# Decode attention: the value product with 128 stationary columns, its lower half added on VectorE, and the last head's inverse issued ahead of the value pages

## The chip, the cores and the metric

One core of one Trainium2 chip runs the whole kernel. The metric is the device time of one execution in microseconds; the median of three runs of the kernel before is 2565.19 us.

## What is computed

One inference step of a small decoder trunk in float32, for a prompt of 1040 rows (1024 and 16 learned ones) and for 8 sequences of 4 new tokens each, called the samples here: a short gated convolution layer with a squared-ReLU MLP, then a layer of attention with forget gates, again with an MLP. The change lies in the attention of the samples. Each sample sequence has 256 cached keys and values in two pages of 128 rows, and 4 new ones:

```python
def forget_attention(q, k, v, c_q, c_k, q_pos, k_pos):
    s = jnp.einsum('nqhd,nkhd->nhqk', q, k, preferred_element_type=jnp.float32) * (HEAD_DIM ** -0.5)
    s = s + (jnp.transpose(c_q, (0, 2, 1))[:, :, :, None] - jnp.transpose(c_k, (0, 2, 1))[:, :, None, :])
    causal = k_pos[None, :] <= q_pos[:, None]
    s = jnp.where(causal[None, None], s, NEG_INF)
    p = jax.nn.softmax(s, axis=-1)
    return jnp.einsum('nhqk,nkhd->nqhd', p.astype(v.dtype), v)
...
past_v = gather_pages(cache_v, page_table)
y = attend(q, ctx).reshape(N, T, ATTN_DIM) @ w_o[j]
```

With 16 heads and 4 queries there are 64 rows of probabilities for each sequence.

## The kernel before, in words

The program is written by hand for each engine, with semaphores between them. Activations stand transposed, features on partitions. TensorE works in the float32r format; to keep accuracy each operand is split into a high part (ScalarE rounds it) and a low part (VectorE subtracts), and a product is made as high by high, low by high and high by low.

**Around the change.** The prompt's attention runs head by head; its last step for a head is to send the sums of the exponentials through memory, to invert them, and to divide. SP does this: `spread_sums` (L1563) spreads the sums over partitions, VectorE inverts them in `invert_sums` (L1279), `load_inverse` stores the inverse (L1570), waits until it is stored, and loads it back broadcast over 64 partitions (L1573). VectorE then divides (`divide`, L1286), ScalarE rounds the result (`o_split_hi`, L1498), VectorE cuts its low part (`o_split_lo`, L1503). After head 15 SP loads the new values, then the two value pages of sequence 0 (`load_v_pages`, L1597), then the inverse of head 15.

After that the output projection of the prompt runs on TensorE: eight units of eight steps, each step six matmuls of 358 columns (L591). Between its steps `decode_step` puts the work of the samples by a table: seven steps are one round. In round n TensorE

- turns the keys of sequence n in four parts (`d_turn_keys`, L1300, four transposes each), at the steps 0, 2 and 4 and, for the last part, between the two halves of the value product;
- turns the probabilities of sequence n-1 at step 2 (`d_turn_probs`, L1415);
- at step 4 multiplies them with the values (`d_weigh`, L1460 and L1462), 512 output columns at a time;
- at step 6 turns the output (`d_turn_out`, L1477) and then makes the logits of sequence n (`d_logits`, L1362 to L1366).

Each part of the keys has one bank: ScalarE rounds it (`d_keys_hi`, L1325), VectorE cuts the low part (`d_keys_lo`, L1330) and so frees the bank for the next part. The logits already use 128 stationary columns, high and low queries side by side; ScalarE copies the lower half of the result (`d_cross`, L1372), and VectorE adds it (L1381) on the way to the maximum (L1383). Then ScalarE takes the exponential (`d_exp`, L1391) and VectorE normalises (`d_norm`, L1398 to L1404).

The probabilities, turned, lie in one PSUM tile as 2 pages and 1 block of new keys, 64 columns each. `d_probs_hi` (L1423) rounds all of it, `d_probs_lo` (L1428, L1432) cuts the low parts. `d_weigh` takes for each page three matmuls (high by high, low by high, high by low) and one for the new keys: seven for a half, 14 for a sequence. `d_keep` (L1469) copies both halves to `d_out`. The value pages are rounded by `d_values_hi` (L1438) and cut by `d_values_lo` (L1445); of the new values the low part is cut at L1892.

**The order on each engine** is that of the code. In rounds 1 to 4 VectorE goes, after the keys of sequence n and the low queries: `add_prompt` (L1964, the sum of the projection's unit into the residual), `cut_unit` (L575, the low part of the weights of the unit after the next), `d_values_lo` (L1445), `d_max`. In rounds 5 to 7 `add_prompt` and `cut_unit` come behind `d_values_lo`. Round 8 only finishes sequence 7. ScalarE goes in rounds 1 to 4: keys, queries, rounding of the weights (L567), `d_keep`, `d_values_hi`, `d_output` (L1491).

Of the kernel before, what the change touches and what calls it, by code (L numbers as in the profile page):

```python
# [215 lines left out]
def trunk(nc, a, out):  # L216

    ctx = ExitStack()
    with ctx:
# [203 lines left out]
        DPL = put("d_probs_t_lo", [P, NPAGE, HQ], F32R)  # L423
# [10 lines left out]
        DPH = put("d_probs_t_hi", [P, NPAGE + 1, HQ], F32R)  # L434
# [78 lines left out]
        dw_done, dw_kept, do_done, do_used = sem("dw_done"), sem("dw_kept"), sem("do_done"), sem("do_used")  # L513
        o_hi, o_lo, rest_hi, rest_lo = sem("o_hi"), sem("o_lo"), sem("rest_hi"), sem("rest_lo")
# [904 lines left out]
        def d_probs_hi(b):  # L1419

            act.wait_ge(dp_done, b + 1)
            ge(act, dw_done, 2 * b)
            act.activation(DPH[:, :, :].rearrange("p g r -> p (g r)"), ps_probs(), ACT.Copy).then_inc(dp_hi, 1)  # L1423

        def d_probs_lo(b):

            dve.wait_ge(dp_hi, b + 1)
            dve.tensor_tensor(DPL[:, :, :].rearrange("p g r -> p (g r)"), ps_probs()[:, 0:NPAGE * HQ],  # L1428
                              DPH[:, 0:NPAGE, :].rearrange("p g r -> p (g r)").bitcast(F32), ALU.subtract)\
               .then_inc(dp_used, 1)  # L1430
            low = DPH[NS:2 * NS, NPAGE, :]
            dve.tensor_tensor(low, ps_probs()[NS:2 * NS, NPAGE * HQ:], low.bitcast(F32), ALU.subtract).then_inc(dp_used, 1)  # L1432
# [15 lines left out]
        def d_weigh(b, h):  # L1448

            if h == 0:  # L1450
                if b == 0:
                    pe.wait_ge(acc_free, 3 * HEADS)
                    pe.wait_ge(vn_lo, 1)
                pe.wait_ge(dv_lo, NPAGE * (b + 1))
                pe.wait_ge(dp_used, 2 * b + 2)
                ge(pe, dw_kept, 2 * b)
            f = slice(512 * h, 512 * h + 512)
            for g in range(NPAGE):
                for n in range(3):
                    pe.matmul(PS[0:HQ, D_OUT + h, :], (DPL if n == 1 else DPH)[:, g], (VPL if n == 2 else VPH)[:, g, f],  # L1460
                              start=(g == 0 and n == 0), stop=False)
            pe.matmul(PS[0:HQ, D_OUT + h, :], DPH[0:3 * NS, NPAGE], VD[:, f], start=False, stop=True).then_inc(dw_done, 1)  # L1462

        def d_keep(b):

            ge(act, do_done, b)
            for h in range(2):
                act.wait_ge(dw_done, 2 * b + h + 1)
                act.activation(OD[:, 512 * h:512 * h + 512], PS[0:HQ, D_OUT + h, :], ACT.Copy).then_inc(dw_kept, 1)  # L1469
# [58 lines left out]
        def attention_loaders(stage_out):  # L1528
# [87 lines left out]
            def prompt_loads():  # L1616
# [24 lines left out]
                for x in range(3):  # L1641
                    sp.dma_start(VN[NS * x:NS * x + NS, :], out["v_sample"].rearrange("b t h d -> (b t) (h d)"))\
                      .then_inc(vn_loaded, 16)
                load_v_pages(0)
                load_inverse(HEADS - 1)
# [76 lines left out]
        def attention_scalar(square, root, inverse, stage_hi):  # L1722
# [57 lines left out]
            d_values_hi(0)  # L1780
# [4 lines left out]
            d_exp(0)  # L1785
            d_keys_hi(1, 1)
# [46 lines left out]
        def attention_vector(head_lo, head_fin, stage_lo):  # L1833
# [56 lines left out]
            dve.wait_ge(vn_hi, 1)  # L1890
            low = VD[2 * NS:3 * NS, :]
            dve.tensor_tensor(low, VN[2 * NS:3 * NS, :], low.bitcast(F32), ALU.subtract).then_inc(vn_lo, 1)  # L1892
# [3 lines left out]
            d_norm(0)  # L1896
            d_values_lo(0, 0)
            d_keys_lo(1, 1)
            d_values_lo(0, 1)
            for n in range(1, DB):  # L1900
# [8 lines left out]
                if n <= 4:  # L1909
                    add_prompt(n - 1)  # L1910
                    cut_unit(U_O + n + 1)
                d_values_lo(n)
# [13 lines left out]
            cut_unit(U_O + DB)  # L1926
            dve.wait_ge(rest_hi, KC + 1)
# [1354 lines left out]
```

## Time and profile before

| | |
|---|---|
| runs | 2564.46, 2565.19, 2565.80 us |
| profiled execution | 2564.02 us, its span 2561.7 us |
| TensorE (PE) matmul busy | 2525.1 us, 99% of the span |
| VectorE (DVE) busy | 1808.4 us, 71% |
| ScalarE (ACT) busy | 1048.2 us, 41% |
| mean granted clock of TensorE | 0.999 of full speed |
| the rounds of the samples | about 1690 to 1830 us |
| value product, L1460 and L1462 | 112 matmuls of 512 columns |

A row of a timeline has its start and its length in us from the start of the span; matmuls overlap in their lengths, so what one costs is read from start to start. "Idle before" names who ended the wait. PE is the matmul side of TensorE and PEld its weight load, which runs ahead of the matmul; SPq is the DMA queue of SyncE.

### The profile page before, as it was taken

The page shows a single profiled execution, that of the slowest core. Times are in us where ns is not written, and L with a number is a line of the kernel's source. Part 1 is how long each engine was busy: PE and PEld are TensorE (multiplying, and loading weights), DVE is VectorE, ACT ScalarE, POOL GpSimd, SP SyncE. Part 2 cuts the span into 40 slices and gives each one's busy share as a digit, 9 for nine tenths or more (in the row PEclk, how much of TensorE's full clock was granted, in tenths as well). Part 3 has the DMA queues.
Part 4 walks back from the last instruction along what each step waited for, and adds up shares of the span by engine and source line. Part 5 has one row for each costly group of instructions (what it writes and reads, how often), then busy time and mean ns, then how long its engine had stood idle before and what let it go on. Part 6 is the DMA issues. An engine that isn't in the chain of part 4 may idle for free.

```text
span 2561.7 us, 45919 instructions
## 1 busy us (share of the span) xinstructions
PE 2525.1 (99%) x18332; PEld 2473.7 (97%) x18332; DVE 1808.4 (71%) x2438; ACT 1048.2 (41%) x1491; POOL 24.4 (1%) x48
## 2 busy tenths in 40 slices
PE   8999999999999999999999999999999999999998
PEld 8999999999999999999999899988899999999998
DVE  5434437666688998954345898876696666899986
ACT  4111124333333323465245777765553333333333
POOL 0000000000000000000000100000000000000000
PEclk9999999999999999999999999999999999999999
DMA  3111111332353312025424656644223333433111
GB/s 120 50 41 48 43 43 40 124 101 101 102 197 105 129 63 90 6 83 168 118 77 137 141 136 167 145 127 148 92 84 101 101 101 108 178 135 135 51 51 69
DMA packets 248430, 259.42 MB, mean 101 GB/s; under 512 B 18160, under 2 KB 182960, under 8 KB 248290
## 3 DMA queue, kind: packets, MB, share of 16 engines
q1 hardware_dynamic: 229030, 248.37, 31.1%
q10 hardware_dynamic: 19260, 9.09, 1.3%
q8 instruction: 100, 1.64, 0.3%
q14 instruction: 40, 0.33, 0.0%
HBM read 193.86 MB, written 63.42 MB: 100 GB/s over the span
## 4 chain that ended last, share of the span: by engine, by line
PE 87%; DVE 4%; DMA 3%; ACT 2%; issue 2%; SPq 2%; ACTq 0%; DVEq 0%
PE ps L591 28%; PE ps L790 24%; PE ps L845 24%; PE ps L810 2%; DMA sums_spread<-o_and_sums 1%; PE ps L1252 1%; PE ps L1102 1%; PE ps L1167 1%; PE ps L1254 1%; PE ps L1253 1%; PE ps L1169 1%; PE ps L1460 1%; PE ps L629 1%; PE ps L692 1%; DMA inv_rows<-inv_spread 0%
## 5 line engine op out<-in xcount | busy, mean ns | idle before, releaser
L845 PE MATMUL ps<-h_op,w_op 128*128 128x268 f32 x4912 | 615.1, 286 | 2.7 <-DVE w_op L885 2.5
L845 PEld LDWEIGHTS ps<-h_op,w_op 128*128 128x128 f32 x4912 | 610.4, 189 | 3.4 <-DVE w_op L885 3.4
L591 PE MATMUL ps<-x_hi,w_hi 128*128 128x358 f32 x1248 | 277.2, 330 | 4.9 <-DVE w_lo L575 4.7
L575 DVE TENSOR_TENSOR w_lo<-w_raw,w_hi 128x1024 fp32r<-128x1024 f32 x76 | 92.8, 1221 | 257.2 <-ACT w_hi L567 257.2
L591 PE MATMUL ps<-x_hi,w_lo 128*128 128x358 f32 x1248 | 273.3, 327 | 0.0
L591 PE MATMUL ps<-x_lo,w_hi 128*128 128x358 f32 x1248 | 272.9, 327 | 0.0
L856 ACT ACTIVATE w_op<-w_op_f 128x2048 fp32r<-128x2048 f32 (+1 forms) x54 | 97.7, 1809 | 388.4 <-PE ps L845 367.6
L591 PEld LDWEIGHTS ps<-x_hi,w_hi 128*128 128x128 f32 x1248 | 213.7, 190 | 7.1 <-DVE w_lo L575 5.1
L591 PEld LDWEIGHTS ps<-x_lo,w_hi 128*128 128x128 f32 x1248 | 215.9, 189 | 0.0
L591 PEld LDWEIGHTS ps<-x_hi,w_lo 128*128 128x128 f32 x1248 | 215.6, 189 | 0.0
L1040 DVE TENSOR_TENSOR t<-ps,t 128x536 f32<-128x536 f32 x180 | 128.7, 715 | 120.2 <-PE ps L790 111.4
L567 ACT ACTIVATE w_hi<-w_raw 128x1024 fp32r<-128x1024 f32 x76 | 80.0, 1054 | 295.2 <-PE ps L591 291.0
L971 DVE TENSOR_TENSOR acc<-ps,acc 128x536 f32<-128x536 f32 x256 | 174.2, 706 | 14.3 <-PE ps L845 13.9
L885 DVE TENSOR_TENSOR h_op<-h_op_f,h_op 128x2144 fp32r<-128x2144 f32 (+1 forms) x56 | 125.9, 2248 | 43.1 <-ACT h_op L856 43.1
L790 PE MATMUL ps<-x_hi,a_lo 128*128 128x268 f32 x720 | 148.3, 287 | 0.0
L790 PE MATMUL ps<-x_T_hi,s_lo 128*128 128x268 f32 x720 | 147.7, 286 | 0.0
L1008 ACT ACTIVATE t<-t 128x536 f32<-128x536 f32 x90 | 58.9, 654 | 184.7 <-DVE t L1014 184.7
L885 DVE TENSOR_TENSOR w_op<-w_op_f,w_op 128x2048 fp32r<-128x2048 f32 (+1 forms) x54 | 115.7, 2142 | 0.0
L790 PEld LDWEIGHTS ps<-x_hi,a_lo 128*128 128x128 f32 x720 | 112.9, 189 | 0.0
L790 PEld LDWEIGHTS ps<-x_T_hi,s_lo 128*128 128x128 f32 x720 | 112.5, 189 | 0.0
L1211 DVE TENSOR_TENSOR probs_lo<-probs_f,probs_hi 128x768 fp32r<-128x768 f32 (+3 forms) x128 | 98.1, 766 | 20.2 <-ACT probs_hi L1199 10.6
L856 ACT ACTIVATE h_op<-h_op_f 128x2144 fp32r<-128x2144 f32 (+1 forms) x56 | 104.5, 1869 | 7.9 <-DVE h_op_f L933 7.8
(358 smaller groups left out, 5173.6 us busy)
## 6 DMA issues: line engine op xcount, KB each, us to landing
raw_a<-in_mlp_w SPq DMA_DIRECT2D x120, 256.0 KB, 3.1
h_op_f<-h_rows SPq DMA_DIRECT2D x24, 1072.0 KB, 6.2
w_op_f<-in_mlp_w SPq DMA_DIRECT2D x24, 1024.0 KB, 7.5
h_rows<-t SPq DMA_DIRECT2D x90, 268.0 KB, 2.1
w_raw<-in_conv_w_in SPq DMA_DIRECT2D x24, 512.0 KB, 3.7
w_raw<-in_w_kv SPq DMA_DIRECT2D x16, 512.0 KB, 4.7
w_raw<-in_w_o SPq DMA_DIRECT2D x16, 512.0 KB, 3.9
k_page<-in_cache_k SPq DMA_DIRECT2D x16, 512.0 KB, 5.1
```

The costliest lines, as they stand in the source:

```text
L567: act.activation(WH[:, s], RAW[:, s], ACT.Copy).then_inc(w_hi, 1)
L575: dve.tensor_tensor(WL[:, s], RAW[:, s], WH[:, s].bitcast(F32), ALU.subtract).then_inc(w_lo, 1)
L591: mm = pe.matmul(PS[:, bank(s, g), 0:GW], w[:, s, k], x[:, k, g * GW:(g + 1) * GW], start=(k == 0 and n == 0), stop=(k == KC - 1 and n == 2))
L790: mm = pe.matmul(PS[:, 2 * p + g, 0:QW], w[:, k], x[:, k, g * QW:(g + 1) * QW], start=(k == 0 and j == 0), stop=(k == KC // 2 - 1 and j == 2))
L810: mm = pe.matmul(PS[:, 2 * p + g, 0:QW], w[:, k, P * m:P * m + P], x[:, k, a:a + QW], start=(k == 0 and j == 0), stop=(k == UNIT_TILES - 1 ...
L845: mm = pe.matmul(PS[:, 2 * p + g, 0:QW], w[:, k, P * m:P * m + P], x[:, k, QW * g:QW * g + QW], start=(k == 0 and j == 0), stop=(k == tile ...
L856: act.activation(h_flat(to, n), h_flat(raw, n), ACT.Copy).then_inc(second_hi, 1)
L885: dve.tensor_tensor(h_flat(pieces[1], n), h_flat(raw, n), h_flat(pieces[0], n).bitcast(F32), ALU.subtract) .then_inc(second_lo, 1)
L971: mm = dve.tensor_tensor(two(to), pair(PAIRS2[l][i]), two(to), ALU.add)
L1008: act.activation(UB[USLOT[q]], UB[USLOT[q]], ACT.Square).then_inc(hf_done, 1)
L1040: dve.tensor_tensor(two(to), pair(p), two(other), ALU.add).then_inc(m_read, 1)
L1211: dve.tensor_tensor(PBL[:, t % HI_RING, 0:nb * w], PF[:, t % 2, 0:nb * w], PBH[:, t % HI_RING, 0:nb * w].bitcast(F32), ALU.subtract).then_ ...
```

## The change

Three things are edited.

1. High and low probabilities of the two pages stand side by side in one tile (`DPT`, 128 columns a page), those of the new keys in a tile of their own (`DPN`). ScalarE rounds them in two instructions where it was one. `d_weigh` takes the high part of a page's values with all 128 columns in one matmul, whose rows 64 to 127 are the low probabilities' share: five matmuls for a half, ten for a sequence.
2. `d_keep` copies rows 64 to 127 instead of rows 0 to 63, and a new `d_sum` on VectorE adds rows 0 to 63 to that copy, for each half of 512 columns. `d_turn_out` waits for it. `d_sum` stands ahead of `d_values_lo` in every round, and behind `add_prompt` and `cut_unit` in rounds 1 to 4 and in round 8.
3. For head 15 `load_inverse` is issued ahead of `load_v_pages(0)`. On ScalarE the rounding of the first pages moves behind the first exponential; on VectorE the cut of the new values' low part (L1892) moves behind the first normalising.

```diff
-        DPL = put("d_probs_t_lo", [P, NPAGE, HQ], F32R)
+        DPN = put("d_probs_t_new", [P, HQ], F32R)
...
-        DPH = put("d_probs_t_hi", [P, NPAGE + 1, HQ], F32R)
+        DPT = put("d_probs_t_hi_lo", [P, NPAGE, 2 * HQ], F32R)
...
         def d_probs_hi(b):
...
-            act.activation(DPH[:, :, :].rearrange("p g r -> p (g r)"), ps_probs(), ACT.Copy).then_inc(dp_hi, 1)
+            act.activation(DPT[:, :, 0:HQ], ps_probs()[:, 0:NPAGE * HQ].rearrange("p (g r) -> p g r", r=HQ), ACT.Copy)\
+               .then_inc(dp_hi, 1)
+            act.activation(DPN[:, :], ps_probs()[:, NPAGE * HQ:], ACT.Copy).then_inc(dp_hi, 1)
...
         def d_weigh(b, h):
...
-            for g in range(NPAGE):
-                for n in range(3):
-                    pe.matmul(PS[0:HQ, D_OUT + h, :], (DPL if n == 1 else DPH)[:, g], (VPL if n == 2 else VPH)[:, g, f],
-                              start=(g == 0 and n == 0), stop=False)
-            pe.matmul(PS[0:HQ, D_OUT + h, :], DPH[0:3 * NS, NPAGE], VD[:, f], start=False, stop=True).then_inc(dw_done, 1)
+            out, pairs = PS[0:HQ, D_OUT + h, :], PS[0:2 * HQ, D_OUT + h, :]
+            pe.matmul(pairs, DPT[:, 0], VPH[:, 0, f], start=True, stop=False)
+            pe.matmul(out, DPT[:, 0, 0:HQ], VPL[:, 0, f], start=False, stop=False)
+            pe.matmul(out, DPT[:, 1, 0:HQ], VPL[:, 1, f], start=False, stop=False)
+            pe.matmul(out, DPN[0:3 * NS, :], VD[:, f], start=False, stop=False)
+            pe.matmul(pairs, DPT[:, 1], VPH[:, 1, f], start=False, stop=True).then_inc(dw_done, 1)
...
         def d_keep(b):
...
-                act.activation(OD[:, 512 * h:512 * h + 512], PS[0:HQ, D_OUT + h, :], ACT.Copy).then_inc(dw_kept, 1)
+                act.activation(OD[:, 512 * h:512 * h + 512], PS[HQ:2 * HQ, D_OUT + h, :], ACT.Copy).then_inc(dw_cross, 1)
+
+        def d_sum(b):
+
+            for h in range(2):
+                dve.wait_ge(dw_cross, 1 + 2 * b + h + 1)
+                x = OD[:, 512 * h:512 * h + 512]
+                dve.tensor_tensor(x, PS[0:HQ, D_OUT + h, :], x, ALU.add).then_inc(dw_kept, 1)
...
+                load_inverse(HEADS - 1)
                 load_v_pages(0)
-                load_inverse(HEADS - 1)
...
             act.activation(VD[:, :], VN[:, :], ACT.Copy).then_inc(vn_hi, 1)
-            d_values_hi(0)
...
             d_exp(0)
+            d_values_hi(0)
...
-            dve.wait_ge(vn_hi, 1)
-            low = VD[2 * NS:3 * NS, :]
-            dve.tensor_tensor(low, VN[2 * NS:3 * NS, :], low.bitcast(F32), ALU.subtract).then_inc(vn_lo, 1)
             o_split_lo(KC - 1)
             d_max(0)
             d_keys_lo(1, 0)
             d_norm(0)
+            dve.wait_ge(vn_hi, 1)
+            low = VD[2 * NS:3 * NS, :]
+            dve.tensor_tensor(low, VN[2 * NS:3 * NS, :], low.bitcast(F32), ALU.subtract).then_inc(vn_lo, 1)
             d_values_lo(0, 0)
...
                 if n <= 4:
                     add_prompt(n - 1)
                     cut_unit(U_O + n + 1)
+                d_sum(n - 1)
                 d_values_lo(n)
...
             cut_unit(U_O + DB)
+            d_sum(DB - 1)
```

The order of VectorE's instructions in rounds 1 to 4, from the cut of the last two parts of the keys (L1330) to the maximum. Before:

```order
L1330 TENSOR_TENSOR k_t_lo<-ps,k_t_hi 128x4x128 x2
L1344 TENSOR_TENSOR q_blocks_hi_lo<-q_all,q_blocks_hi_lo 64x8x4 x2
L1346 SCALAR_TENSOR_TENSOR sums_lo<-past_sums,sums_hi 16x288
L1964 TENSOR_TENSOR acc<-ps,acc 128x716
L575 TENSOR_TENSOR w_lo<-w_raw,w_hi 128x1024
L1445 TENSOR_TENSOR v_page_lo<-v_page,v_page_hi 128x2048
L1381 TENSOR_TENSOR mask_and_cross<-mask_row,d_cross 64x288
```

The same place with the change (its line numbers are its own):

```order
L1331 TENSOR_TENSOR k_t_lo<-ps,k_t_hi 128x4x128 x2
L1345 TENSOR_TENSOR q_blocks_hi_lo<-q_all,q_blocks_hi_lo 64x8x4 x2
L1347 SCALAR_TENSOR_TENSOR sums_lo<-past_sums,sums_hi 16x288
L1976 TENSOR_TENSOR acc<-ps,acc 128x716
L576 TENSOR_TENSOR w_lo<-w_raw,w_hi 128x1024
L1479 TENSOR_TENSOR d_out<-ps,d_out 64x512 x2
L1447 TENSOR_TENSOR v_page_lo<-v_page,v_page_hi 128x2048
```

Two sums (L1479) stand between the cut of the weights and the cut of the value pages.

TensorE between the turning of the keys and the turning of the output (`d_out`), with the change; before, each half had seven matmuls of 64 stationary columns:

```order
L1461 MATMUL ps<-v_page_hi,d_probs_t_hi_lo 128x512
L1462 MATMUL ps<-v_page_lo,d_probs_t_hi_lo 64x512
L1463 MATMUL ps<-v_page_lo,d_probs_t_hi_lo 64x512
L1464 MATMUL ps<-v_new_hi_hi_lo,d_probs_t_new 64x512
L1465 MATMUL ps<-v_page_hi,d_probs_t_hi_lo 128x512
L1301 MATMUL ps<-ident,k_page 128x128 x4
```

The first and last matmul of a half now write 128 rows; the last turning of the keys still stands between the halves.

VectorE from the division of the last heads (L1286) to the value pages, before:

```order
L1286 TENSOR_TENSOR q_all<-o_and_sums,inv_sums 64x1040 x2
L1892 TENSOR_TENSOR v_new_hi_hi_lo<-v_new,v_new_hi_hi_lo 32x1024
L1503 TENSOR_TENSOR hid_lo<-q_all,hid_hi 128x716
L1381 TENSOR_TENSOR mask_and_cross<-mask_row,d_cross 64x288
...
L1404 TENSOR_SCALAR d_probs<-d_probs,d_stats 64x288
L1445 TENSOR_TENSOR v_page_lo<-v_page,v_page_hi 128x1024
```

and with the change:

```order
L1287 TENSOR_TENSOR q_all<-o_and_sums,inv_sums 64x1040 x2
L1513 TENSOR_TENSOR hid_lo<-q_all,hid_hi 128x716
L1382 TENSOR_TENSOR mask_and_cross<-mask_row,d_cross 64x288
...
L1405 TENSOR_SCALAR d_probs<-d_probs,d_stats 64x288
L1906 TENSOR_TENSOR v_new_hi_hi_lo<-v_new,v_new_hi_hi_lo 32x1024
L1447 TENSOR_TENSOR v_page_lo<-v_page,v_page_hi 128x1024
```

The cut of the new values has moved from ahead of L1503 to behind the normalising.

## Rows read from the trace of the kernel before

**Rows 1.** Waits, 1680 to 1850 us: who waited, total us, times, longest

```profile
PE ps L591 <- DVE hid_lo L1503: 3.0, 2, 2.7
PEld ps L1300 <- DVE k_t_lo L1330: 2.0, 7, 0.3
```

**Rows 2.** Timeline of TensorE, round 2: start us, length us, instruction

```profile
1729.54 0.39 PE L1462 MATMUL ps<-v_new_hi_hi_lo,d_probs_t_hi 96*64 96x512 f32 x1
1729.77 0.62 PE L1300 MATMUL ps<-ident,k_page 128*128 128x128 f32 x4
...
1731.61 0.40 PE L1462 MATMUL ps<-v_new_hi_hi_lo,d_probs_t_hi 96*64 96x512 f32 x1
...
1733.91 0.71 PE L1477 MATMUL ps<-ident,d_out 64*128 64x64 f32 x8
```

**Rows 3.** Timeline of VectorE, round 2

```profile
1728.98 0.69 DVE L1330 TENSOR_TENSOR k_t_lo<-ps,k_t_hi 128x512 fp32r<-128x512 f32 x1 [1.29 <-ACT k_t_hi L1325]
...
1732.70 0.88 DVE L1964 TENSOR_TENSOR acc<-ps,acc 128x716 f32<-128x716 f32 x1
1733.52 1.20 DVE L575 TENSOR_TENSOR w_lo<-w_raw,w_hi 128x1024 fp32r<-128x1024 f32 x1
```

**Rows 4.** Timeline of ScalarE, round 2

```profile
1728.35 0.60 ACT L1325 ACTIVATE k_t_hi<-ps 128x512 fp32r<-128x512 f32 x1 [2.10 <-PE ps L1300]
...
1732.71 1.05 ACT L1469 ACTIVATE d_out<-ps 64x512 f32<-64x512 f32 x2
1733.67 1.90 ACT L1438 ACTIVATE v_page_hi<-v_page 128x2048 fp32r<-128x2048 f32 x1
```

**Rows 5.** Timeline of SP's DMA queue: stores and loads of the inverses, heads 14 and 15

```profile
1686.69 0.35 SPq L1570 DMA_DIRECT2D inv_rows<-inv_spread  x1
1688.04 0.48 SPq L1573 DMA_DIRECT2D inv_sums<-inv_rows  x1
...
1695.33 0.44 SPq L1570 DMA_DIRECT2D inv_rows<-inv_spread  x1
1699.45 0.48 SPq L1573 DMA_DIRECT2D inv_sums<-inv_rows  x1
```

**Rows 6.** The value pages' tile: time of their 16 loads

```profile
DMA to landing us min/median/max: 3.2/5.1/5.7
```

**Rows 7.** Timeline of VectorE, ahead of round 1

```profile
1693.90 0.23 DVE L1279 RECIPROCAL inv_spread<-sums_spread 65x16 f32<-65x16 f32 x1
...
1699.64 1.23 DVE L1286 TENSOR_TENSOR q_all<-o_and_sums,inv_sums 64x1040 f32<-64x1040 f32 x1
1702.84 1.24 DVE L1286 TENSOR_TENSOR q_all<-o_and_sums,inv_sums 64x1040 f32<-64x1040 f32 x1 [1.97 <-DMA inv_sums<-inv_rows]
1704.00 1.21 DVE L1892 TENSOR_TENSOR v_new_hi_hi_lo<-v_new,v_new_hi_hi_lo 32x1024 fp32r<-32x1024 f32 x1
1705.24 0.91 DVE L1503 TENSOR_TENSOR hid_lo<-q_all,hid_hi 128x716 fp32r<-128x716 f32 x1
...
1712.79 0.69 DVE L1330 TENSOR_TENSOR k_t_lo<-ps,k_t_hi 128x512 fp32r<-128x512 f32 x1
```

**Rows 8.** Timeline of TensorE, ahead of round 1 and in it

```profile
1706.20 0.59 PE L591 MATMUL ps<-hid_hi,w_hi 128*128 128x358 f32 x2 [2.73 <-DVE hid_lo L1503]
...
1713.78 0.60 PE L1300 MATMUL ps<-ident,k_page 128*128 128x128 f32 x4
```

**Rows 9.** Timeline of TensorE, rounds 5 and 6

```profile
1777.81 0.62 PE L1300 MATMUL ps<-ident,k_page 128*128 128x128 f32 x4
...
1781.98 0.71 PE L1477 MATMUL ps<-ident,d_out 64*128 64x64 f32 x8
...
1789.64 0.36 PE L1415 MATMUL ps<-ident,d_probs 64*128 64x64 f32 x3 [0.21 <-DVE d_probs L1404]
```

**Rows 10.** Start of the kernel: TensorE's timeline, and the busy-time table (last: clock, DMA)

```profile
21.71 1.23 PE L591 MATMUL ps<-x_hi,w_hi 128*128 128x358 f32 x3 [4.47 <-DVE w_lo L575]
...
20.00:30.00 10.00, 8.29 (x41) 8.29 (x42) 10.00 (x11) 8.92 (x10) 0.00 (x0) 0.83 0.19 54
```

More of the change, by code:

```diff
@@ L513, in trunk @@
         dw_done, dw_kept, do_done, do_used = sem("dw_done"), sem("dw_kept"), sem("do_done"), sem("do_used")
+        dw_cross = lt_kept
         o_hi, o_lo, rest_hi, rest_lo = sem("o_hi"), sem("o_lo"), sem("rest_hi"), sem("rest_lo")
@@ L1422, in d_probs_hi @@
             ge(act, dw_done, 2 * b)
-            act.activation(DPH[:, :, :].rearrange("p g r -> p (g r)"), ps_probs(), ACT.Copy).then_inc(dp_hi, 1)
+            act.activation(DPT[:, :, 0:HQ], ps_probs()[:, 0:NPAGE * HQ].rearrange("p (g r) -> p g r", r=HQ), ACT.Copy)\
+               .then_inc(dp_hi, 1)
+            act.activation(DPN[:, :], ps_probs()[:, NPAGE * HQ:], ACT.Copy).then_inc(dp_hi, 1)
         def d_probs_lo(b):
[L1427 to L1431, printed above, removed]
+            dve.wait_ge(dp_hi, 2 * b + 2)
+            dve.tensor_tensor(DPT[:, :, HQ:2 * HQ], ps_probs()[:, 0:NPAGE * HQ].rearrange("p (g r) -> p g r", r=HQ),
+                              DPT[:, :, 0:HQ].bitcast(F32), ALU.subtract).then_inc(dp_used, 1)
+            low = DPN[NS:2 * NS, :]
             dve.tensor_tensor(low, ps_probs()[NS:2 * NS, NPAGE * HQ:], low.bitcast(F32), ALU.subtract).then_inc(dp_used, 1)
```

## Prediction

> **What bounds the kernel now.** I started from the busy shares on the page: TensorE is busy nearly all the time, so a matmul taken out looks like time gained. That is an average, though, so I went to the one stretch that the change touches, from about 1690 to 1830 us, and read there first the list of waits, then the timelines of the engines side by side. The waits show two things [rows 1]. TensorE waits once for long, 2.7 us for the low half of head 15's output (L1503). And its weight loader waits seven times 0.3 us at L1300 for the low half of the keys (L1330): once a round, hidden under a running matmul, so with no slack left behind it. I call "round n" the seven steps in which TensorE weighs the values of sequence n-1 and turns the keys of sequence n; T is the start of the round's last turning of keys (L1300 between the two halves of the value product). T is 1729.77 in round 2 and 1777.81 in round 5 [rows 2, 9].
>
> **Part 1: fewer matmuls in the value product.** Seven matmuls of 512 columns per half become five; 2 x 2 x 8 = 32 go. One takes 0.23 us: from the last of a half at 1729.54 to the L1300 behind it at 1729.77 [rows 2]. On TensorE alone that is 32 x 0.23 = 7.4 us. Where do they lie?
>
> *First half, rounds 1 to 7.* L1300 at T needs the bank that L1330 frees. In round 2 ScalarE rounds the turning before it from 1728.35, L1330 runs 1728.98 to 1729.67, and T is 1729.77 [rows 2 to 4]. TensorE's own product ended exactly then. With two matmuls less TensorE is there 0.46 us earlier and waits 0.46 us for the same L1330. T does not move: gain 0. (Two matmuls by 0.23 are hidden by the chain ScalarE, VectorE; without that chain they would be worth 0.46 us a round.)
>
> *Second half, rounds 1 to 7.* It shortens the way from T to the turning of the output (L1477), which then stands at a new wait, part 2.
>
> *Round 8* has no keys to turn; its four removed matmuls count in full, 4 x 0.23 = 0.93 us, since the new adds are covered there: ScalarE's copy of half a row block (1.05 us for two, [rows 4]) and one add (0.69) make some 1.3 us against the 2.3 us between the last value matmul, 1731.61, and L1477, 1733.91 [rows 2]. **-0.9 us.**
>
> **Part 2: the added sum on VectorE.** ScalarE now copies the low rows (same size, same place in its order), and VectorE adds the high rows, twice 64 x 512 out of PSUM; only then may L1477 start. The trace has no such add. The nearest row is L1330, also 512 elements with one side in PSUM: 0.69 us [rows 3]. Two, with the 0.06 us by which neighbours overlap (L1964 starts at 1732.70, takes 0.88, and L575 starts at 1733.52), are 1.32 us. Bounds: 1.1 and 1.5 us.
>
> What counts is where VectorE takes them. In rounds 1 to 4 the order puts them behind the prompt's sum (L1964) and the cut of the next weights (L575), ahead of the value pages. L575 starts at T + 3.75 and takes 1.20 [rows 3]; the sums run from T + 4.88 to T + 6.20, and L1477 follows some 0.1 us later, at **T + 6.3**. Today it is at T + 4.14 [rows 2], right behind ScalarE's copies (1732.71 plus 1.05, that is T + 3.99, [rows 4]). TensorE would be ready at T + 3.6, so the new wait is 2.7 us, and the round gets 6.3 - 4.14 = 2.17 us longer. Everything behind hangs on L1477: the logits of the next sequence, their maximum, exponential, the turned probabilities. VectorE's pages (L1445) are done before the slipped logits, so they cost nothing. **4 x 2.17 = +8.7 us.**
>
> In rounds 5 to 7 the order has neither L1964 nor L575 ahead. VectorE is free at T + 2.93 (where L1964 starts in round 2), the sums end at T + 4.25 and L1477 starts at T + 4.4 instead of 4.17 (1781.98, [rows 9]): +0.2. Rounds 5 and 6 hide that: there the maximum stands behind the pages, L1964 and L575, which start from ScalarE and not from L1477, and TensorE already waits 0.21 us for the probabilities at 1789.64 [rows 9]. Round 7 does not. **+0.2 us.**
>
> The split of the probabilities costs ScalarE a second copy of 64 columns, about 0.2 us, ahead of the 2.10 us for which it is idle before L1325 at 1728.35 [rows 4]. The price is 0 while that gap stands, and 0.2 us a round if it closed.
>
> **Part 3: head 15's inverse first.** Today SP issues two value pages, then stores the inverse at 1695.33, which returns only at 1699.45; one head earlier, with nothing in front, the same store took 1686.69 to 1688.04, 1.35 us [rows 5]. The inverse is made at 1693.90 to 1694.13 [rows 7]. So: store 1694.2, load issued 1695.6, landed 3.4 us later as today (1699.45 to 1702.84), at 1699.0. VectorE takes it behind head 14's division, which starts at 1699.64 and takes 1.23: head 15's runs 1700.8 to 1702.0 instead of 1702.84 to 1704.08. ScalarE's L1498 and L1503 follow: L1503 at 1703.0 instead of 1705.24, where 0.2 us was also spent behind L1892, now moved [rows 7]. TensorE's 2.7 us wait [rows 1, 8] shrinks by 2.2.
>
> But the value product is late next. L1892 (1.21 us, with overlap 1.13) moves behind the normalising, into the unbroken row of VectorE work that leads to L1330 at 1712.79 and so to T of round 1, 1713.78 [rows 7, 8]. From L1503 to L1330 it was 7.55 us, it becomes 8.68. L1330 then starts at 1711.7 and ends at 1712.4, T is at 1712.5. The pages are issued from 1696.1 on and take up to 5.7 us to land [rows 6]. ScalarE now rounds them behind the exponential; with 1.90 us for it [rows 4] it must start by 1705.5, when L1503 is at 1703.0 and VectorE's first page at 4.5 us behind it. They are there in time. **-1.3 us.** Bounds: if the store still takes 4.1 us, L1503 gains 1.3 and T only 0.3; L1503 could gain 2.5 at most, T then 1.5.
>
> **Sum:** 8.7 + 0.2 - 0.9 - 1.3 = **+6.7 us**. It is made against the profiled execution, 2564.02 us (a span of 2561.7); the median of the runs is 1.2 above it, so I forecast 2565.2 + 6.7 = **2571.9 us**. What the measurement can tell from no change is about 0.2%, 5.1 us. With all bounds (sums 1.1 to 1.5 each round, part 3 from -0.3 to -1.5) the forecast's own range is 2570.6 to 2574.
>
> A weighing of a page: the trace gives 0.23 us for a 512-column matmul with its own weights [rows 2]. The Trainium skill, "TensorE: Matmul & The Clock Gate", section "Back-to-back issue gap", gives about 131 ns for such pairs in a sustained stream; by it the 32 matmuls would be 4.2 us and the sum +7.1 instead of +6.7. The trace disagrees, so I stay with it.
>
> **Rivals.**
> *A, faster: the matmuls count.* If VectorE's sums were done by T + 3.6, TensorE would never wait at L1477, and if L1330 came earlier too, all 32 matmuls would count: -7.4, with the inverse's -1.3 2556.5 us. The point that decides is the end of L575 at T + 4.9, which would have to fall ahead of T + 2.3. Against it stands the unbroken row of VectorE from T + 2.9 [rows 3]. Chance 0.07.
> *B, no change that can be told: T moves.* If the freed 0.46 us of the first half does come through in rounds 1 to 5 (L1330 having some slack that the trace hides), 5 x 0.46 = 2.3 go off: +4.4, 2569.6 us. Against it: the seven waits of the loader [rows 1]. Chance 0.15.
> *C, slower still: late pages.* The pages are now behind the inverse's load and in front of 1 MB of weights. Should they land 2 us later than ScalarE wants them, T of round 1 loses that: 2574 us. Chance 0.1.
> *D, the clock.* Idle of 4.47 us at the start of the kernel was followed by the lower level: granted clock 0.83 over 20 to 30 us, so 10 x 0.17 = 1.7 us lost [rows 10]. The wait of 2.73 us at 1706.20 was followed by matmuls at the usual pace, 0.59 us for the first pair [rows 8]; 1.23 us was taken by three after the long idle [rows 10]. The new waits are as long as that one, 2.7 us. If each of four were punished, +6.8: 2578.7 us. Chance 0.05. [...]
>
> **How the numbers follow.** The forecast has 0.63, B 0.15, C 0.1, D 0.05, A 0.07. B's time is within 0.2%, as is the low tail of the forecast (0.03): same 0.18. Slower: 0.60 + 0.1 + 0.05 = 0.75. Faster: 0.07. The range of 8 in 10 leaves out A and D, reaches down to B with its tolerance, 2568.5, and up to C, 2575.
>
> **What would show it.** In the profile after: the sum's VectorE row at about 0.69 us, 16 of them; TensorE's L1477 (there L1487) waiting for VectorE in rounds 1 to 4, 2.7 us each, some 11 to 12 in total, and about 0.8 each in 5 to 7; a wait at L1300 of about 0.46 us a round; rounds 1 to 4 at 18.2 us from T to T where 16.0 was; the wait at L1503 down to about 0.5 us, and a wait of over 1 us ahead of round 1's value product. A granted clock below 1.00 in 1715 to 1780 would mean D. Wrong altogether is the prediction if L1477 shows no wait for VectorE, or if the T to T of rounds 2 to 4 is 16 us or less.

## The result: slower by more than forecast

| kernel | median us (lowest to highest, runs) | against before |
|---|---|---|
| before | 2565.16 (2564.46 to 2569.96, 6) | |
| changed | 2576.49 (2574.16 to 2581.47, 6) | 1.0045 [1.0034, 1.0057] |

The change costs 11.3 us where +6.7 was forecast; 2576.5 lies above the range (2568.5 to 2575). Of the changed kernel the profiled execution took 2574.16 us.

The page of the changed kernel: TensorE is busy 2.0 us less than before although the span is 10.1 us longer.

```profile
span 2571.8 us, 45879 instructions
PE 2523.1 (98%) x18300; PEld 2472.3 (96%) x18300; DVE 1818.1 (71%) x2454; ACT 1049.8 (41%) x1499; POOL 24.4 (1%) x48
```

Where TensorE waits in the rounds (waits, 1680 to 1860 us: total, times, longest), changed kernel. Beside [rows 1] the long wait for head 15 is gone (L1513, 0.5 at most), and the turning of the output (L1487, before L1477) waits for the sums of VectorE:

```profile
PEld ps L1487 <- DVE d_out L1479: 12.6, 6, 2.8
PE ps L1487 <- DVE d_out L1479: 10.8, 6, 2.5
PE ps L1301 <- DVE k_t_lo L1331: 2.0, 7, 0.5
PE ps L1461 <- DVE d_probs_t_new L1434: 1.0, 1, 1.0
PE ps L592 <- DVE hid_lo L1513: 0.8, 2, 0.5
```

TensorE's timeline, changed kernel: the wait of 0.36 us near the end of the prompt's attention (L1253, before L1252), whose end I use as a mark since nothing above it was changed; then T of rounds 1 to 3 (L1301) and the turning of the output (L1487) of each. They answer to [rows 2, 8].

```profile
1689.28 0.40 PE L1253 MATMUL ps<-probs_hi,v_hi 128*128 128x272 f32 x1 [0.36 <-DVE probs_lo L1212]
...
1714.17 0.66 PE L1301 MATMUL ps<-ident,k_page 128*128 128x128 f32 x4
1720.40 0.71 PE L1487 MATMUL ps<-ident,d_out 64*128 64x64 f32 x8 [2.45 <-DVE d_out L1479]
...
1732.21 0.66 PE L1301 MATMUL ps<-ident,k_page 128*128 128x128 f32 x4 [0.25 <-DVE k_t_lo L1331]
1738.46 0.71 PE L1487 MATMUL ps<-ident,d_out 64*128 64x64 f32 x8 [2.44 <-DVE d_out L1479]
...
1751.77 0.65 PE L1301 MATMUL ps<-ident,k_page 128*128 128x128 f32 x4 [0.25 <-DVE k_t_lo L1331]
1758.01 0.71 PE L1487 MATMUL ps<-ident,d_out 64*128 64x64 f32 x8 [2.45 <-DVE d_out L1479]
```

Read two things. From T to L1487 it is 6.2 us in rounds 1 to 4 (before 4.1). But from T to T it is 18.04 in round 1 and 19.56 in round 2, with the same wait in both; rounds 3 and 4 are 18.07 and 19.55. The table of busy times over the 6 us behind each of the four waits (the last three columns are granted clock, DMA share, GB/s) tells the two kinds apart:

```profile
1720.00:1726.00 6.00, 5.60 (x41) 5.07 (x42) 3.55 (x5) 1.80 (x8) 0.20 (x1) 1.00 0.94 313
1738.00:1744.00 6.00, 5.54 (x30) 4.70 (x31) 2.60 (x2) 1.07 (x6) 0.00 (x0) 0.72 0.94 268
1758.00:1764.00 6.00, 5.99 (x43) 5.46 (x44) 3.34 (x5) 1.82 (x7) 0.20 (x1) 1.00 0.98 323
1776.00:1782.00 6.00, 5.92 (x32) 5.11 (x33) 2.44 (x3) 0.91 (x5) 0.00 (x0) 0.72 0.98 327
```

In rounds 2 and 4 the granted clock fell (mean 0.72; in the middle of these stretches 0.50, which is the 1.2 GHz level), and 30 and 32 matmul records lie where 41 and 43 do at 1.00. Such a fall costs 19.55 - 18.06 = **1.5 us**.

The sums by stretches, each end a row of TensorE's timeline (mark L1252/L1253 at 1687.94 before and 1689.28 after; o8 is the output's turning in round 8, 1829.40 and 1840.35):

| stretch | before | changed | forecast | measured |
|---|---|---|---|---|
| mark to T of round 1 | 25.84 | 24.89 | -1.3 | -0.95 |
| T of round 1 to T of round 5 | 64.03 | 75.22 | +8.7 | +11.19, of which 2 x 1.5 clock |
| T of round 5 to T of round 7 | 32.82 | 32.94 | 0 | +0.12 |
| T of round 7 to o8 | 18.77 | 18.02 | +0.2 - 0.9 | -0.75 |
| sum | 141.46 | 151.07 | +6.7 | +9.61 |

Without the clock it is +6.6. The mark itself comes at 1687.9 to 1691.2 us over the 14 profiles of this study, in code that none of the kernels changes; the stretches from the mark on leave that scatter out, the medians hold it.

### The profile page after: what moved, and what is told of

Same layout as the page of the kernel before. It is cut to its first block, busy times and chain, and to the rows that moved or that the text cites. A ratio compares the mean times of both kernels' runs of the same rounds, so it can differ in the third digit from the quotient of the medians.

```text
span 2571.8 us, 45879 instructions
## 1 busy us (share of the span) xinstructions
PE 2523.1 (98%) x18300; PEld 2472.3 (96%) x18300; DVE 1818.1 (71%) x2454; ACT 1049.8 (41%) x1499; POOL 24.4 (1%) x48
## 4 chain that ended last, share of the span: by engine, by line
PE 86%; DVE 4%; ACT 3%; DMA 2%; issue 2%; SPq 1%; ACTq 0%; DVEq 0%
PE ps L592 27%; PE ps L791 24%; PE ps L846 23%; PE ps L811 2%; PE ps L1253 1%; DMA sums_spread<-o_and_sums 1%; PE ps L1103 1%; PE ps L1168 1%; PE ps L1255 1%; PE ps L1254 1%; PE ps L1170 1%; PE ps L630 1%; PE ps L693 1%; DVE x_lo L610 0%; DMA tokens_in<-in_x_prompt 0%
## 5 line engine op out<-in xcount | busy, mean ns | idle before, releaser
L846 PE MATMUL ps<-h_op,w_op 128*128 128x268 f32 x4912 | 615.0, 286 | 2.7 <-DVE w_op L886 2.5
L846 PEld LDWEIGHTS ps<-h_op,w_op 128*128 128x128 f32 x4912 | 610.4, 189 | 3.4 <-DVE w_op L886 3.4
```

Of the source, the lines that this page charges most:

```text
L846: mm = pe.matmul(PS[:, 2 * p + g, 0:QW], w[:, k, P * m:P * m + P], x[:, k, QW * g:QW * g + QW], start=(k == 0 and j == 0), stop=(k == tile ...
```

## The experiments

"Theory W" in the expectations below is the view that the loss is TensorE's wait for the sums, made by the order in VectorE's queue, together with the clock's falls behind that wait; "theory M" puts the loss on the merged product itself. What the result leaves open is whether the rest, 3 us in this profile and up to 5 in the medians, is the clock, and whether the clock falls because TensorE idles.

### Where VectorE takes the sums: sum_first, keep_first

```diff
# sum_first, VectorE (its order changes in rounds 1 to 4)
+                d_sum(n - 1)
                 if n <= 4:
                     add_prompt(n - 1)
                     cut_unit(U_O + n + 1)
-                d_sum(n - 1)
...
# keep_first, on top, ScalarE
+                d_keep(n - 1)
                 if n <= 4:
                     round_unit(U_O + n + 1)
-                d_keep(n - 1)
```

sum_first: 

> The changed kernel with the two sums ahead of the prompt's sum and the cut of the weights in rounds 1 to 4 (VectorE's order alone; nothing else is edited). Theory W (the loss is TensorE's wait for the sums behind those two instructions, and after a wait of 2.4 us the clock sometimes falls): ScalarE's second copy still ends at about T + 4.2, the sum behind it at T + 4.9, so the output's turning starts at T + 5.0 instead of T + 6.2; the wait shrinks from 2.45 to about 1.2 us, the clock of 1720 to 1800 us is 1.00 in every stretch, and the time is 4 x 1.2 + 3 = 8 us less than the changed kernel, some 2568 us, 2 to 3 above the kernel before. Theory M (the loss is in the product itself: matmuls of 128 columns, or what they do to the clock): the order of VectorE matters little, 2574 to 2577 us, and stretches at 0.5 remain.

keep_first: 

> As the run before, and ScalarE copies the halves ahead of rounding the next weights in rounds 1 to 4. Theory W: all rounds are like rounds 5 to 7 of the changed kernel; the output's turning at T + 4.3, wait 0.5 us, clock 1.00; against the kernel before 7 x 0.15 more, 0.9 less in round 8 and 1.0 less at the start: 2564 to 2565 us, the same as before within 0.1%. Theory M: 2572 us or more.

Measured: sum_first 2564.94 us (ratio 1.0002 [0.9993, 1.0011]), keep_first 2562.47 (0.9991 [0.9982, 1.0000]). Moving one call brings the time back to that of the kernel before. TensorE's output turnings of rounds 1 and 2 in sum_first, then of round 2 in keep_first:

```profile
1719.16 0.71 PE L1487 MATMUL ps<-ident,d_out 64*128 64x64 f32 x8 [1.27 <-DVE d_out L1479]
...
1736.05 0.71 PE L1487 MATMUL ps<-ident,d_out 64*128 64x64 f32 x8 [1.28 <-DVE d_out L1479]
```

```profile
1733.70 0.71 PE L1487 MATMUL ps<-ident,d_out 64*128 64x64 f32 x8 [0.50 <-DVE d_out L1479]
```

The wait falls from 2.45 to 1.27 to 0.50 us, the rounds from 18.06 to 16.9 and 16.12 us (16.01 before), and in both kernels the clock stays at 1.00 through all rounds. So sum_first's rounds are still 0.9 us longer than before; the gains of parts 1 and 3 pay for most of that. sum_first came out some 3 us under its expectation, keep_first some 2. From the mark to o8 sum_first takes 143.45 us, 2.0 above before; outside, its mark comes 1.3 us later and the stretch behind o8 is 2.6 us shorter, in part because its profile has no fall behind the late wait of L846 where the profile of before has one (L845, below). How much of the 3 us in the medians that explains, no run shows.

### Part 3: start_as_before, start_alone

start_as_before is the changed kernel without part 3, start_alone the kernel before with part 3 only; the diffs are part 3 of the change, backwards and forwards.

start_as_before: 

> The changed kernel without the part at the start: pages ahead of head 15's inverse, the first pages' rounding and the new values' cut where they were. Theory W: the waits of rounds 1 to 4 stay at 2.4 us and so does the clock's fall; only the 1.0 us that T of round 1 gained is lost, 2577 to 2578 us. Rival S (the start's reordering does harm, a wait of over 1 us ahead of the first value product): faster than the changed kernel by 1 us or more, 2575 or less.

start_alone: 

> The kernel before with the part at the start alone. Theory W: T of round 1 comes 1.0 us earlier (my sum said 1.3), nothing after it changes: 2564.2 us. Rival S: the same or slower, since the value product waits for the cut of the new values; 2565.5 or more.

Measured: 2579.57 us (1.0056 [1.0042, 1.0069]) and 2563.51 (0.9993 [0.9984, 1.0002]). By the medians part 3 is a gain of 1.6 us alone, with an interval that takes in no gain, and of 3.1 us within the change (0.4 beside the changed kernel's second set of runs, below), so they do not settle its size. The profiles do it better. Alone, the stretch from the mark to the output's turning of round 1 is 29.26 us where it was 29.96, so -0.7. Within the change it can save more than that, since a fall of the clock can follow the wait that it shortens too, here in start_as_before (timeline, and the busy times of 1706 to 1716 us with a granted clock of 0.66):

```profile
1708.46 0.97 PE L592 MATMUL ps<-hid_hi,w_hi 128*128 128x358 f32 x2 [3.02 <-DVE hid_lo L1513]
```

```profile
1706.00:1716.00 10.00, 7.54 (x31) 6.99 (x32) 7.87 (x16) 3.34 (x8) 0.21 (x1) 0.66 0.46 150
```

The first pair takes 0.97 us where it took 0.59 behind nearly the same wait in the kernel before [rows 8]. From the mark to T it is 28.15 us, 2.3 more than before. The same wait is 3.38 us in wait_alone (below), and there too the granted clock over 1706 to 1716 us is 0.83. So of the three profiles with a long wait for head 15 two had a fall behind it (3.02 and 3.38 us), and the kernel before, at 2.73 us, had none.

### The product alone: no_sum

no_sum keeps the merged product and leaves the sums out, so the share of the low probabilities is missing from its output.

```diff
-                act.activation(OD[:, 512 * h:512 * h + 512], PS[HQ:2 * HQ, D_OUT + h, :], ACT.Copy).then_inc(dw_cross, 1)
+                act.activation(OD[:, 512 * h:512 * h + 512], PS[0:HQ, D_OUT + h, :], ACT.Copy).then_inc(dw_kept, 1)
...
-                d_sum(n - 1)
...
-            d_sum(DB - 1)
```

> The changed kernel without the added sums on VectorE: ScalarE copies rows 0 to 63, so the share of the low probabilities is left out of the output; the product keeps its five matmuls per half. Theory W (the loss is the wait for the sums, and the 32 removed matmuls are worth next to nothing since T hangs on the low half of the keys): -1.0 from the earlier inverse, -0.9 from round 8, about 0 from the other rounds, so 2563.2 us (2562 to 2564), rounds of 16.0 us from T to T. Rival A (all 32 matmuls count): 2565.1 - 7.4 - 1.0 = 2556.7 us.

Measured: 2561.64 us (0.9987 [0.9978, 0.9996]), 1.6 below the expected figure and 5 above rival A's. From the mark to o8 it is 138.50 us, 2.96 less than before: 0.95 at the start, 0.69 from T of round 1 to T of round 7 (0.12 a round), 1.32 behind that. So the 32 removed matmuls give 2.0 us of their 7.4: I had 0.9. Rounds of 15.9 us show the binding: TensorE now waits at T for L1331 (0.25 in its rows, rounds 2 to 7) and, in rounds 1 to 4, 0.29 at the output's turning for ScalarE's copy. This kernel is also the measure of what the sums cost: 14.9 us in the changed kernel, 3.3 in sum_first, 0.8 in keep_first.

### The wait alone, and a longer one

wait_alone keeps the kernel before, with its seven matmuls a half, and adds on VectorE, at the place of the sums, a maximum over each half of the product; nobody reads the result, but the output's turning waits for it. longer_wait adds such a maximum ahead of each sum of the changed kernel.

```diff
# wait_alone
...
-                act.activation(OD[:, 512 * h:512 * h + 512], PS[0:HQ, D_OUT + h, :], ACT.Copy).then_inc(dw_kept, 1)
+                act.activation(OD[:, 512 * h:512 * h + 512], PS[0:HQ, D_OUT + h, :], ACT.Copy).then_inc(dw_cross, 1)
...
+        def d_sum(b):
...
+            for h in range(2):
+                dve.wait_ge(dw_cross, 1 + 2 * b + h + 1)
+                dve.tensor_reduce(SCR[:, h:h + 1], PS[0:HQ, D_OUT + h, :], mybir.AxisListType.X, ALU.max)\
+                   .then_inc(dw_kept, 1)
...
+                d_sum(n - 1)
...
+            d_sum(DB - 1)
...
# longer_wait, in d_sum of the changed kernel
+                dve.tensor_reduce(SCR[:, h:h + 1], PS[0:HQ, D_OUT + h, :], mybir.AxisListType.X, ALU.max)
```

wait_alone: 

> The kernel before, with its product of seven matmuls, and on VectorE, at the place of the added sums, two maxima over the same 64 x 512 in PSUM (their result goes nowhere) for which the turning of the output waits. Output unchanged. Theory W: the wait alone makes the loss. The matmuls were not shortened, so TensorE waits some 2.0 us at L1477 instead of 2.45, L1477 is at T + 6.1 to 6.3, rounds 1 to 4 are 18.0 to 18.2 us: 2565.1 + 4 x 2.1 + 0.2 = 2573.7 us if the clock stays, up to 2579.7 if it falls in each of four rounds (1.5 each). A rival that puts the loss on the merged product itself (its 128 rows, or the mix of tile sizes): 2565 us.

longer_wait: 

> The changed kernel with a maximum over 64 x 512 in PSUM (result unused) ahead of each of the added sums on VectorE. Each should take about 0.6 us, so the wait at the turning of the output grows from 2.45 to about 3.7 us and rounds 1 to 4 by 1.2 each, rounds 5 to 7 by 1.2 at most: 2576.5 + 5 + 2 to 3.6. Theory that the length of the wait sets whether the clock falls: it falls in all four rounds (2 of 4 in the profile of the changed kernel), 2 x 1.5 more, so 2586 to 2588 us. If the falls are set by something else, 2 of 4 again: 2583.5 to 2585 us.

Measured: wait_alone 2577.99 us (1.0055 [1.0041, 1.0068]), longer_wait 2593.76 (1.0106 [1.0092, 1.0120]). The merged product is not to blame: the old product with the wait loses 12.8 us, the changed kernel 11.3. The four stretches behind the waits, first of wait_alone (waits of 2.0 us), then of longer_wait (3.65 us):

```profile
1722.00:1728.00 6.00, 5.92 (x32) 5.27 (x33) 2.46 (x3) 0.91 (x5) 0.00 (x0) 0.72 1.01 307
1742.00:1748.00 6.00, 6.00 (x35) 5.10 (x33) 2.41 (x3) 0.91 (x5) 0.00 (x0) 0.72 0.97 321
1761.00:1767.00 6.00, 5.79 (x42) 5.26 (x43) 3.34 (x6) 1.61 (x7) 0.20 (x1) 1.00 0.96 285
1779.00:1785.00 6.00, 5.73 (x31) 4.91 (x32) 2.44 (x3) 0.91 (x5) 0.00 (x0) 0.72 0.89 292
```

```profile
1723.00:1729.00 6.00, 6.00 (x33) 5.24 (x34) 2.41 (x2) 0.91 (x5) 0.00 (x0) 0.72 0.92 301
1744.00:1750.00 6.00, 6.00 (x35) 5.33 (x34) 2.42 (x3) 0.91 (x5) 0.00 (x0) 0.72 0.93 300
1764.00:1770.00 6.00, 5.44 (x30) 4.81 (x31) 2.71 (x2) 0.81 (x5) 0.00 (x0) 0.72 0.94 311
1785.00:1791.00 6.00, 5.74 (x26) 4.74 (x26) 2.41 (x2) 0.50 (x4) 0.00 (x0) 0.52 0.96 308
```

Three falls of four in the one, four of four in the other, as expected of a cause that grows with the wait. Part of wait_alone's time is the fall behind its wait for head 15: from the mark to T it takes 1.6 us more than before. longer_wait is 6 to 8 us slower than I expected: the fourth fall is longer than the others, and its clock falls again at the end of rounds 6 and 7, behind waits of 1.9 and 1.7 us, which I had not counted (granted clock 0.66 over 1824 to 1834 and over 1844 to 1854 us). The wait of 1.7 us in round 5 had no fall.

### The wait without the idle: wait_filled, after_again

```diff
         def d_turn_out(b):
 
+            if b < 4:
+                pe.wait_ge(ds_used, b + 1)
+                for m in range(16):
+                    pe.matmul(PS[:, D_ROWS, 0:KEYS], HH[:, 0, 0:P], HH[:, 0, 0:KEYS], start=True, stop=True)
             pe.wait_ge(dw_kept, 2 * b + 2)
```

wait_filled: 

> The changed kernel with 16 matmuls of 288 columns on TensorE ahead of its wait at the turning of the output, in rounds 1 to 4. They write columns that the logits write anew right behind, so the output is unchanged; at 0.13 us each (as the logits' own) they fill 2.1 of the 2.45 us of idle and end before the sums do. Theory that the loss has two parts, the wait for the sums (2.05 a round) and a clock that falls because TensorE idled: the rounds stay 18.05 us, the granted clock stays 1.00 in all four, and the kernel takes 2565.2 + 8.2 + 0.2 - 0.9 - 1.0 = 2571.7 us (2570.5 to 2572.5), against 2576.5. Rival that the falls have another cause than the idle time: 2576 us again, windows at 0.5 after some of the rounds.

after_again: 

> The changed kernel once more, unchanged, for a second profile of its clock. If which rounds are followed by a fall is chance, it is another set than rounds 2 and 4; if it is a property of the place, rounds 2 and 4 again. Median 2576.5 us as before (2574 to 2579).

Measured: wait_filled 2570.82 us (1.0019 [1.0010, 1.0028]), after_again 2579.20 (1.0047 [1.0033, 1.0060]), both beside the same runs of before (2565.78). This is the run that decides. Round 2 of wait_filled (timeline), and its stretches behind the four waits:

```profile
1734.53 2.27 PE L1486 MATMUL ps<-hid_hi 128*128 128x288 f32 x16
1737.14 0.71 PE L1491 MATMUL ps<-ident,d_out 64*128 64x64 f32 x8 [0.34 <-DVE d_out L1479]
```

```profile
1719.00:1725.00 6.00, 5.92 (x43) 5.39 (x44) 3.34 (x6) 1.74 (x7) 0.20 (x1) 1.00 0.94 313
1737.00:1743.00 6.00, 5.86 (x43) 5.33 (x43) 3.33 (x6) 1.68 (x7) 0.20 (x1) 1.00 1.00 319
1755.00:1761.00 6.00, 5.79 (x42) 5.26 (x43) 3.34 (x6) 1.62 (x7) 0.20 (x1) 1.00 0.97 298
1773.00:1779.00 6.00, 5.75 (x42) 5.21 (x43) 3.33 (x6) 1.56 (x8) 0.20 (x1) 1.00 0.97 304
```

And the changed kernel's second profile:

```profile
1722.00:1728.00 6.00, 5.65 (x31) 5.00 (x32) 2.49 (x2) 0.99 (x6) 0.00 (x0) 0.72 0.90 296
1742.00:1748.00 6.00, 6.00 (x34) 5.06 (x35) 2.47 (x2) 0.91 (x5) 0.00 (x0) 0.72 0.95 306
1761.00:1767.00 6.00, 5.56 (x41) 5.03 (x42) 3.50 (x5) 1.56 (x7) 0.21 (x1) 1.00 0.92 298
1780.00:1786.00 6.00, 6.00 (x33) 5.11 (x32) 2.41 (x3) 0.91 (x5) 0.00 (x0) 0.72 1.02 335
```

The sums come as late (the output's turning is again 6.24 us behind T, 18.06 from one to the next), TensorE does 16 matmuls more in each of the four rounds, and the kernel is 5.7 to 8.4 us faster than the changed one, by the two sets of runs; the slowest of its 11 runs (2573.25) is under the fastest of the changed kernel's 11 (2573.93). Only TensorE's idle time was filled, and the falls went with it: that the idle time brings them on is shown. The changed kernel had two falls in its first profile and three in its second: the same code does not fall in the same rounds, though round 3 was spared both times, and in wait_alone and start_as_before too. Why round 3, no run tells.

### Taking the product's gain: product_whole, product_whole_2, whole_and_new_first

product_whole is keep_first with these moves; product_whole_2 is the same kernel once more; whole_and_new_first also puts L1906 back to where L1892 stood.

```diff
                     d_weigh(n - 1, 0)
-                    if n < DB:
-                        d_turn_keys(n, 3)
                     d_weigh(n - 1, 1)
+                    if n < DB:
+                        d_turn_keys(n, 3)
# ScalarE; on VectorE d_sum moves the same way ahead of d_keys_lo(n, 3)
+                d_keep(n - 1)
                 d_keys_hi(n, 3)
                 d_queries_hi(n)
-                d_keep(n - 1)
```

product_whole: 

> The kernel keep_first with both halves of the value product in one go and the last turning of keys behind them (TensorE), ScalarE's copies and VectorE's sums of the product ahead of that turning's halves. It takes away TensorE's wait for the low half of the keys at T (0.46 us of TensorE's time a round) and the 0.50 us left at the turning of the output. Theory W: these two are all that stands between the removed matmuls and a gain, so rounds 1 to 4 get 0.9 us shorter, 15.2 us, rounds 5 to 7 up to 0.9: 2562.5 - 3.6 - 0 to 2.7 = 2556.5 to 2559 us. Rival: the chain behind the logits (maximum, exponential, the turned probabilities) binds next, and TensorE waits there for what it gained: 2561 to 2562.5 us.

product_whole_2: 

> The kernel product_whole once more, unchanged. Its profile had a fall of the clock behind the 1.0 us wait ahead of round 1's value product, worth about 1.5 us. 2558.0 us (2556.5 to 2559.5); without that fall in the profile it would be a span about 1.5 us shorter.

whole_and_new_first: 

> The kernel product_whole with VectorE's low half of the new values (L1906, 1.22 us) back between head 15's division and L1513, where it stood in the kernel before. VectorE idles 0.95 us there, so it costs 0.25 at L1513 and takes 1.22 us out of the row of work ahead of round 1's value product, where TensorE waits 1.0 us: 0.7 to 0.9 us earlier, and one cause less for a fall of the clock: 2557.2 us (2555.5 to 2558). Rival: VectorE's row ahead of T is set by ScalarE's value pages, then no gain: 2558 us.

Measured: product_whole 2557.99 us (0.9968 [0.9956, 0.9981]) and, again, 2559.77 (0.9974 [0.9965, 0.9983]); whole_and_new_first 2558.86 (0.9974 [0.9964, 0.9984]). TensorE no longer waits at the output's turning at all; two of them, rounds 2 and 3, 15.20 us apart, from product_whole_2's timeline:

```profile
1734.05 0.71 PE L1487 MATMUL ps<-ident,d_out 64*128 64x64 f32 x8
...
1749.25 0.71 PE L1487 MATMUL ps<-ident,d_out 64*128 64x64 f32 x8
```

The first rounds are 15.2 us, 0.8 under before, as expected; from round 5 on next to nothing is gained (16.2 and 16.4 us from turning to turning, before 16.2 and 16.6). There the rival holds, the chain behind the logits: TensorE waits 0.50 us for the normalised probabilities (L1405) and 0.3 to 0.5 for L1331. This version beats both kernels, by 0.26 to 0.32% against before. Its first profile had a fall behind a wait of 1.02 us, its second not. The medians of product_whole_2 and whole_and_new_first lie 0.3 and 0.9 us above the ranges expected. whole_and_new_first can't be told from product_whole: the wait of 1.02 us ahead of round 1's value product stayed, and only 0.3 us came off between the mark and that product. The rival named there holds: VectorE's pages, with L1906 out of the way, wait for ScalarE to round them (timeline of VectorE, whole_and_new_first):

```profile
1710.59 1.23 DVE L1447 TENSOR_TENSOR v_page_lo<-v_page,v_page_hi 128x1024 fp32r<-128x1024 f32 x1 [0.83 <-ACT v_page_hi L1440]
```

## Why the prediction was wrong

- **Part 2, the queue on VectorE: right.** Two sums take 1.27 us (forecast 1.32), in the place the order gives them. VectorE's timeline in round 2, changed kernel, beside [rows 3]:

```profile
1735.18 0.88 DVE L1976 TENSOR_TENSOR acc<-ps,acc 128x716 f32<-128x716 f32 x1
1736.00 1.20 DVE L576 TENSOR_TENSOR w_lo<-w_raw,w_hi 128x1024 fp32r<-128x1024 f32 x1
1737.13 1.27 DVE L1479 TENSOR_TENSOR d_out<-ps,d_out 64x512 f32<-64x512 f32 x2
1738.33 2.27 DVE L1447 TENSOR_TENSOR v_page_lo<-v_page,v_page_hi 128x2048 fp32r<-128x2048 f32 x1
```

  L1487 came at T + 6.25 (forecast 6.3), the wait is 2.45 us (2.7), a round without a fall +2.05 us (2.17). That the queue is the cause is shown by sum_first and wait_alone.
- **Part 1, the matmuls: nearly right.** 2.0 us of 7.4 come through (no_sum), 0.9 was forecast; in the changed kernel -0.75 from T of round 7 to o8, as summed. T hung on L1331 as said: in rounds 2 to 7 the rows show a wait of 0.25 us there. From the last value matmul to T it is 0.63 us from start to start (1731.58 to 1732.21 in round 2) where 0.23 stands without a wait, so 0.4 of the 0.46 us freed was lost again.
- **Part 3: right.** -0.95 us at T where -1.3 was forecast. The store of the inverse was issued at 1695.50 and its load at 1696.79 (1.3 us, not 4.1), and L1503, there L1513, came 15.14 us behind the mark (forecast 15.1). The 0.3 us missing at T are VectorE's row from there to L1331, 9.0 us where 8.68 was forecast. start_alone gave 0.7: the rest, 0.25, is part 1, since T there stands 1.65 us behind the first value matmul and 1.41 in the changed kernel. The value product waited 1.01 us for the probabilities, as forecast. L1906 stood ahead of VectorE's pages (1707.88 to 1709.10), but ScalarE had rounded those only at 1708.65, so without it the pages could start some 0.5 us earlier, not 1.2, an estimate from these rows. The pages were in time (ScalarE took them without a wait at 1706.75; rival C did not happen).
- **Rival D, the clock: this is the step that failed.** The sum put the clock's price behind four new waits of 2.7 us at nothing. I gave the rival 0.05, outside the range, on the ground that one wait of 2.73 us had no fall behind it [rows 8]. It happened behind two of the four new waits in one profile and three in the other, at 1.5 us each (forecast 1.7). One execution says little about a thing that comes in some executions and not in others. And the same profile held the counter-example, at its end, where I had not looked because the change is elsewhere: 18 matmuls of L845 behind a wait of 2.52 us. First before, then no_sum (there L846), from the timelines:

```profile
2532.94 3.57 PE L845 MATMUL ps<-h_op,w_op 128*128 128x268 f32 x18 [2.52 <-DVE w_op L885]
```

```profile
2533.08 2.50 PE L846 MATMUL ps<-h_op,w_op 128*128 128x268 f32 x18 [2.52 <-DVE w_op L886]
```

  The granted clock there was 0.83 over 2530 to 2540 us in the kernel before and 1.00 in no_sum. Over the 14 profiles this wait is always 2.52 or 2.53 us; four had no fall (2.5 us for the 18), ten had (3.2 to 4.0). Had I looked, the one profile I had would have shown a fall behind one of two such waits. Four new waits at that share and 1.5 us are +3.0: a forecast of 2574.9 us, and with all four +6.0 a range that takes in the measured time.

  Nor is it only waits of that length. A wait of 1.33 us for L2641 (`k_work`) at about 1417 us stands in all 14 profiles; behind it five had a fall (sum_first, start_alone, longer_wait, after_again, product_whole_2). And at about 1676 us two short waits, 0.8 and 0.55 us with 0.3 us of work between them, stand in all 14, and two had a fall behind them. First start_as_before with a fall, then the changed kernel without:

```profile
1676.51 1.66 PE L2065 MATMUL ps<-ident,logf_page 128*16 128x128 f32 x8 [0.55 <-ACT q_hi_ext L1142]
```

```profile
1677.49 1.03 PE L2065 MATMUL ps<-ident,logf_page 128*16 128x128 f32 x8 [0.55 <-ACT q_hi_ext L1142]
```

What remains: the changed kernel's median is 11.3 over before (13.4 in the second set of runs), 6.6 for wait, matmuls and inverse, and 3.0 to 4.5 for the falls that its two profiles show. wait_filled puts the falls at 5.7 to 8.4 us by the medians, more than 3 x 1.5, and sum_first says the same: 11.6 us less than the changed kernel, of which its shorter rounds are 4 x 1.17 = 4.7. The unprofiled runs may have more or longer falls (the mean clock of those beside the first profile is 0.993 to 0.996, the profiled run's 0.997); that is argued, not shown.

The Trainium skill, "TensorE: Matmul & The Clock Gate", section "HAM oscillation — how this bites in real kernels", warns that idle gaps put TensorE back at half rate, but means gaps longer than any of the four new waits; by it the clock would have stayed. The traces disagree: the granted clock fell behind 8 of the 12 waits of 2.45 us (three profiles). The measurement decides.

## What to carry to other kernels

An operation added to a queue costs what stands ahead of it in that queue: ask for its place before its length. Here two sums of 0.67 us a round cost 14.9 us behind two unrelated operations, 3.3 ahead of them, and 0.8 with ScalarE's copies moved ahead too, each against the kernel without the sums. And a new wait of TensorE has a second price, a fall of its clock, that comes in some executions and not in others: look for every wait of that length in the whole trace, count how often the granted clock falls behind it, and put that share times its price into the sum. Where a wait can't be removed, it can be filled.

## What the runs showed of the hardware

- Falls behind waits of TensorE, of all such waits in rounds 1 to 4: 0.34 us (filled) none of 4; 0.50 none of 4; 1.27 none of 4; 2.0 three of 4; 2.45 eight of 12; 3.65 four of 4. Elsewhere: 1.02 us ahead of round 1's value product, one of 11; 1.33 at about 1417 us, five of 14; 1.35 at about 428 us (L669), none of 14; 2.52 at L845, ten of 14; 0.8 and 0.55 close together, two of 14. So the share differs from place to place too, not by length alone; why is not shown. A fall cost 1.5 us in a round.
- Sixteen matmuls of 288 columns with results nobody reads take 2.27 us and, put into a wait of 2.45, keep the clock at 1.00: more work on TensorE made the kernel faster, by 5.7 to 8.4 us in the medians.
- On VectorE a sum of 64 x 512 with one side in PSUM and a maximum over the same take the same time, 0.67 us (16 each).
